# Hybrid attention block: the column factors of the attention output are applied in the output projection, with a longer probability ring and another step order

## What is computed

```python
def forgetting_attention(q, k, v, f_logit):      # "FoX": 8 heads of width 64
    c = cumsum(log_sigmoid(f_logit))
    s = q @ k.T * scale + c_i - c_j              # causal mask
    p = softmax(s); o = p @ v

def differential_attention(q, k, v, lam, g_sub, lam_init):   # 4 heads, values of width 128
    p1, p2 = softmax(q1 @ k1.T * scale + alibi), softmax(q2 @ k2.T * scale + alibi)
    o = (p1 - lam * p2) @ v
    o = rmsnorm(o, g_sub) * (1 - lam_init)

proj = rmsnorm(x, g_pre_mix) @ w_in              # q, k, v, forget logits of both kinds
mix = concat([fox, diff]) @ w_out
x = x + rmsnorm(mix, g_post_mix)
h = rmsnorm(x, g_pre_mlp)
x = x + rmsnorm(square(relu(h @ w_up)) @ w_down, g_post_mlp)
```

## Time and profile before

| | us |
|---|---|
| median of 3 runs | 3205.31 |
| the profiled execution, its time | 3201.39 |
| its span from the first to the last instruction | 3199.6 |
| PE busy in the span | 2935.2 (92%) |
| DVE busy | 1651.2 (52%) |
| POOL busy | 1030.2 (32%) |
| ACT busy | 1019.4 (32%) |
| mean granted TensorE clock | 0.963 |

### The profile page before, as it was taken

The page is one execution under the profiler, slowest core; times in us unless marked ns, Lnnn a source line. Parts: engine busy times, 40 slices in busy tenths (PEclk is TensorE's granted clock), DMA queues, the critical chain, the costliest instruction groups (busy, mean ns, idle before and its releaser), DMA issues. The chain is left out here.

```text
span 3199.6 us, 39104 instructions
## 1 busy us (share of the span) xinstructions
PE 2935.2 (92%) x13954; PEld 2420.8 (76%) x13954; DVE 1651.2 (52%) x2475; ACT 1019.4 (32%) x1974; POOL 1030.2 (32%) x734
## 2 busy tenths in 40 slices
PE   7999999688788798797797999999999999999996
PEld 5888888577677677676686788888887788888885
DVE  5111111379588588597454444444446544444446
ACT  4111111377577586585222111111112111111111
POOL 4220110158267267366111321222224322222224
PEclk9999999899899899899898999999999999999998
DMA  5342332744643644531663111101116111111112
GB/s 166 125 151 99 118 125 99 143 100 89 108 93 71 115 94 109 68 78 27 211 206 108 60 53 52 44 35 52 52 39 236 66 53 52 52 38 40 52 54 104
DMA packets 234969, 291.27 MB, mean 91 GB/s; under 512 B 37664, under 2 KB 160800, under 8 KB 234848
## 3 DMA queue, kind: packets, MB, share of 16 engines
q1 hardware_dynamic: 179984, 221.55, 26.9%
q10 hardware_dynamic: 54096, 67.38, 5.9%
q0 software_dynamic: 768, 0.79, 0.1%
HBM read 204.77 MB, written 84.90 MB: 91 GB/s over the span
## 5 line engine op out<-in xcount | busy, mean ns | idle before, releaser
L1873 DVE TENSOR_TENSOR ml_y<-ml_y,ml_ps_y 128x512 f32<-128x512 f32 x512 | 351.8, 687 | 233.6 <-PE ml_ps_y L1933 228.7
L1929 PE MATMUL ml_ps_y<-ml_dn_hi,ml_u_hi 128*128 128x512 f32 x1024 | 403.8, 394 | 11.5 <-DVE ml_y L1873 11.5
L1908 PE MATMUL ml_ps_u<-h_rows_hi,ml_up_hi 128*128 128x512 f32 x1024 | 400.0, 391 | 14.4 <-POOL ml_up_lo L1726 14.4
L1933 PE MATMUL ml_ps_y<-ml_dn_hi,ml_u_lo 128*128 128x512 f32 x1024 | 400.3, 391 | 0.0
L1931 PE MATMUL ml_ps_y<-ml_dn_lo,ml_u_hi 128*128 128x512 f32 x1024 | 399.9, 391 | 0.0
L1910 PE MATMUL ml_ps_u<-h_rows_lo,ml_up_hi 128*128 128x512 f32 x1024 | 399.7, 390 | 0.0
L1911 PE MATMUL ml_ps_u<-h_rows_hi,ml_up_lo 128*128 128x512 f32 x1024 | 399.5, 390 | 0.0
L1173 DVE TENSOR_REDUCE at_nmax<-at_ps_s 128x1 f32<-128x1024 f32 (+7 forms) x384 | 345.5, 907 | 83.0 <-PE at_ps_s L1272 77.4
L1849 DVE TENSOR_TENSOR ml_relu<-ml_relu 128x512 f32<-128x512 f32 x128 | 92.3, 721 | 496.6 <-ACT ml_relu L1812 496.6
L1726 POOL TENSOR_TENSOR ml_up_lo<-ml_up_raw,ml_up_hi 128x1024 fp32r<-128x1024 f32 x64 | 166.6, 2619 | 507.2 <-ACT ml_up_hi L1792 507.2
L1733 POOL TENSOR_TENSOR ml_dn_lo<-ml_dn_raw,ml_dn_hi 128x1024 fp32r<-128x1024 f32 x64 | 153.1, 2414 | 534.1 <-ACT ml_dn_hi L1802 534.1
(11 more groups left out here) (206 smaller groups left out, 5702.0 us busy)
## 6 DMA issues: line engine op xcount, KB each, us to landing
qk<-pj_out_sb ACTq DMA_DIRECT2D x64, 512.0 KB, 2.8
ml_up_raw<-in_w_up_dram SPq DMA_DIRECT2D x32, 1024.0 KB, 5.6
ml_dn_raw<-in_w_down_dram SPq DMA_DIRECT2D x32, 1024.0 KB, 7.6
at_q<-qk SPq DMA_DIRECT2D x96, 256.0 KB
at_k<-qk SPq DMA_DIRECT2D x96, 256.0 KB
vals<-pj_out_sb ACTq DMA_DIRECT2D x32, 512.0 KB, 3.0
at_v_sb<-vals SPq DMA_DIRECT2D x32, 512.0 KB, 8.1
pj_raw<-in_w_in_dram SPq DMA_DIRECT2D x24, 512.0 KB, 4.0
```

What stands on the lines that cost most here:

```text
L1873: dve.tensor_tensor(y[:, t, cols], y[:, t, cols], ps_y[:, b % 4, :], ALU.add)\
L1908: pe.matmul(ps_u[:, b % 4, :], up_hi[:, k, cols], h_hi[:, k, rows], start=(k == 0), stop=False)
L1929: pe.matmul(ps_y[:, b % 4, :], u_hi[:, s, f, rows], dn_hi[:, f, cols], start=(f == 0), stop=False)
L1933: last = pe.matmul(ps_y[:, b % 4, :], u_lo[:, s, f, rows], dn_hi[:, f, cols], start=False, stop=(f == FT - 1))
```

## The change

The multiplication by the column factors leaves `attend` and goes to `mix_out`. In `attend` the steps `row_in` and `o_scale` are gone, with the buffer `recips`. `store` is now made per block and not per pair (48 and not 32; a FoX block stores 64 partitions), right after its `o_add`; the ring `o_sb` has 2 slots, one per block, so `o_add` of block n waits for the store of block n - 2. `row_out` stays; the stage's end waits for its last writes. The memory that came free makes the probability ring 153 tiles long. The planner has a new table of urgencies and a new assumed cost of `fix`. In `mix_out`, per tile, three more loads bring the factors of 128 columns, spread over the partitions (512 KB in pieces of 512 bytes), into a single buffer, and DVE multiplies `m_raw` by them before the split.

```diff
-PROB_COLUMNS = 141 * 128
+PROB_COLUMNS = 153 * 128
-ORING = 3
+ORING = 2
-RUSH = {"score": -1.22, "max": -0.39, "corr": 0.1, "exp": 0.11, "fix": 0.34, "chain": -0.49, "mix": 0.53,
-        "turn": 0.12, "hi": 0.1, "lo": -0.23, "pv": 0.25}
-SPREAD, LEAD, EARLY = 1.06, 0.49, 0.72
+RUSH = {"score": -1.03, "max": -0.49, "corr": 0.43, "exp": 0.12, "fix": -0.47, "chain": 0.18, "mix": 0.47,
+        "turn": 0.12, "hi": -0.17, "lo": 0.04, "pv": 0.25}
+SPREAD, LEAD, EARLY = 1.14, 0.49, 1.63
...
-        finish([b], urgency)
-    def finish(pair, urgency):
-        q = pair[0].qb
-        walk.step("row_in", q, "SP", 0.6, urgency, ...)
-        walk.step("o_scale", q, "POOL", 1.3, urgency, [("row_in", q)] + [("o_add", b) for b in pair])
-        walk.step("store", q, "SP", 0.6, urgency, [("o_scale", q)], 6.0, line=("store", q % ORING))
...
-                walk.step("fix", (b.n, sc.a), "POOL", 2.0, at + RUSH["fix"], ...)
+                walk.step("fix", (b.n, sc.a), "POOL", 2.4, at + RUSH["fix"], ...)
...
         walk.step("o_add", b, "DVE", 0.69, end, [("o_half" if fox else "o_sq", b),
-                                                ("store", b.qb - ORING) if b.qb >= ORING else None])
-        if fox and b.s == 1:
-            finish([blocks[b.n - 1], b], end)
+                                                ("store", blocks[b.n - ORING]) if b.n >= ORING else None])
+        walk.step("store", b, "SP", 0.6, end, [("o_add", b)], 8.0, line=("store", b.n % ORING))
...
                 elif what == "store":
+                    b, cols = arg, slice(512 * arg.J, 512 * arg.J + 512)
+                    height = 64 if b.kind == FOX else P
+                    to = mixT[b.i, b.s * 64:b.s * 64 + 64, cols] if b.kind == FOX else mixT[b.i + 4, :, cols]
+                    sp.wait_ge(o_free, b.n + 1)
+                    sp.dma_start(to, o_sb[0:height, b.n % ORING, :]).then_inc(o_stored[b.n % ORING], 16)
...
+            for s in range(4):
+                sp.wait_ge(row_out[s], 16 * (len(blocks) // 4))
...
-                elif what == "o_scale":
-                    pool.wait_ge(row_in[q % 2], 16 * (q // 2 + 1))
-                    pool.wait_ge(o_free, pairs[q][-1].n + 1)
-                    pool.tensor_tensor(o_sb[:, q % ORING, :], o_sb[:, q % ORING, :], recips[:, q % 2, :], ALU.mult)
```

and in `mix_out`:

```diff
+            def load_factors(cols):
+                for half in range(2):
+                    sp.dma_start(factors[64 * half:64 * half + 64, 0:4], col_rows[0:4, half, cols].unsqueeze(0)
+                                 .to_broadcast([64, 4, P])).then_inc(factors_loaded, 16)
+                sp.dma_start(factors[:, 4:8], col_rows[4:8, 0, cols].unsqueeze(0).to_broadcast([P, 4, P]))\
+                  .then_inc(factors_loaded, 16)
+
+            load_mix(0, slice(0, P))
+            load_factors(slice(0, P))
             for k in range(KT):
                 sp.dma_start(w_raw[k], w_out[0, k * P:(k + 1) * P, :]).then_inc(w_loaded[k], 16)
...
+            load_mix(1, slice(P, 2 * P))
+            sp.wait_ge(m_scaled, 1)
+            load_factors(slice(P, 2 * P))
             sp.dma_start(xin[:, 1, :], x[0, P:2 * P, :]).then_inc(x_loaded[1], 16)
             with sp.Fori(0, LAST - 1) as i:
                 for s in range(2):
                     t = 2 * i + s + 2
                     sp.wait_ge(m_ready, t + 1)
+                    load_mix(s, bass.ts(t, P))
+                    sp.wait_ge(m_scaled, t)
+                    load_factors(bass.ts(t, P))
                     sp.wait_ge(y_step, 2 * (t - 1))
                     sp.dma_start(xin[:, s, :], x[0, bass.ts(t, P), :]).then_inc(x_loaded[s], 16)
...
             def split_mix(i, s, t):
                 dve.wait_ge(m_loaded[s], 16 * (i + 1))
+                dve.wait_ge(factors_loaded, 48 * (t + 1))
+                dve.tensor_tensor(m_raw[:, s], m_raw[:, s], factors[:, :, :], ALU.mult).then_inc(m_scaled, 1)
+                dve.wait_ge(m_scaled, t + 1)
                 dve.wait_ge(multiplied, t + 1)
                 dve.tensor_copy(m_hi[:, s], m_raw[:, s]).then_inc(m_hi_ready, 1)
```

More of the change, by code:

```diff
@@ L741, in attention_steps @@
             if sc.part and (fox or sc.s == 0):
-                walk.step("fix", (b.n, sc.a), "POOL", 2.0, at + RUSH["fix"], [("corr", sc), ("exp", parts[0])])
+                walk.step("fix", (b.n, sc.a), "POOL", 2.4, at + RUSH["fix"], [("corr", sc), ("exp", parts[0])])
             if not fox and sc.s == 1 and sc.part == sc.parts - 1:
@@ L798, in attend @@
     places, former = probability_columns(blocks)
-    pairs = [[b for b in blocks if b.qb == q] for q in range(blocks[-1].qb + 1)]
-    col_rows = nc.dram_tensor("col_rows", [KT, 2, S], F32).ap()
     fox_no = {b.n: n for n, b in enumerate(b for b in blocks if b.kind == FOX)}
@@ L900, in attend @@
         o_half_ready = r.sem("o_half_ready")
-        row_in = [r.sem(f"row_in{n}") for n in range(2)]
         o_free = r.sem("o_free")
-        o_scaled = r.sem("o_scaled")
         o_squared = r.sem("o_squared")
@@ L979, in _ @@
                       .then_inc(row_out[n % 4], 16)
[L980 to L991, removed]
-                elif what == "store":
[L993 to L996, removed]
+                elif what == "store":
+                    b, cols = arg, slice(512 * arg.J, 512 * arg.J + 512)
[3 more added lines that the diff above has]
+                    sp.dma_start(to, o_sb[0:height, b.n % ORING, :]).then_inc(o_stored[b.n % ORING], 16)
             for s in range(ORING):
-                sp.wait_ge(o_stored[s], 16 * ((len(pairs) + ORING - 1 - s) // ORING))
+                sp.wait_ge(o_stored[s], 16 * ((len(blocks) + ORING - 1 - s) // ORING))
+            for s in range(4):
+                sp.wait_ge(row_out[s], 16 * (len(blocks) // 4))
         @block.gpsimd
@@ L1319, in _, with mix_out @@
                     last.then_inc(x_ready, 1)
-def mix_out(nc, mixT, w_out, x, g_post_mix, g_pre_mlp, x2, h2T, rows_hi, rows_lo):
+def mix_out(nc, mixT, col_rows, w_out, x, g_post_mix, g_pre_mlp, x2, h2T, rows_hi, rows_lo):
     with ExitStack() as ctx:
@@ L1329, in mix_out @@
         m_raw = r.sb("m_raw", [P, 2, KT, P])
+        factors = r.sb("factors", [P, KT, P])
         m_hi = r.sb("m_hi", [P, 2, KT, P], F32R)
@@ L1351, in mix_out @@
         m_loaded = [r.sem(f"m_loaded{s}") for s in range(2)]
+        factors_loaded = r.sem("factors_loaded")
         x_loaded = [r.sem(f"x_loaded{s}") for s in range(2)]
+        m_scaled = r.sem("m_scaled")
         m_hi_ready = r.sem("m_hi_ready")
@@ L1376, in _, with load_mix @@
         def _(sp):
-            sp.dma_start(m_raw[:, 0], mixT[:, :, 0:P].rearrange("k p n -> p k n")).then_inc(m_loaded[0], 16)
+            def load_mix(s, cols):
+                sp.dma_start(m_raw[:, s], mixT[:, :, cols].rearrange("k p n -> p k n")).then_inc(m_loaded[s], 16)
+            def load_factors(cols):
[6 more added lines that the diff above has]
+            load_factors(slice(0, P))
             for k in range(KT):
@@ L1382, in _ @@
             sp.dma_start(xin[:, 0, :], x[0, 0:P, :]).then_inc(x_loaded[0], 16)
-            sp.dma_start(m_raw[:, 1], mixT[:, :, P:2 * P].rearrange("k p n -> p k n")).then_inc(m_loaded[1], 16)
+            load_mix(1, slice(P, 2 * P))
+            sp.wait_ge(m_scaled, 1)
+            load_factors(slice(P, 2 * P))
             sp.dma_start(xin[:, 1, :], x[0, P:2 * P, :]).then_inc(x_loaded[1], 16)
@@ L1388, in _ @@
                     sp.wait_ge(m_ready, t + 1)
-                    sp.dma_start(m_raw[:, s], mixT[:, :, bass.ts(t, P)].rearrange("k p n -> p k n"))\
-                      .then_inc(m_loaded[s], 16)
+                    load_mix(s, bass.ts(t, P))
+                    sp.wait_ge(m_scaled, t)
+                    load_factors(bass.ts(t, P))
                     sp.wait_ge(y_step, 2 * (t - 1))
@@ L1954, in hybrid_block @@
         rows_lo = r.sb("rows_lo", [P, KT, S // 2], F32R)
-        mix_out(nc, mixT, w_out, x, g_post_mix, g_pre_mlp, x2, h2T, rows_hi, rows_lo)
+        mix_out(nc, mixT, col_rows, w_out, x, g_post_mix, g_pre_mlp, x2, h2T, rows_hi, rows_lo)
         mlp(nc, rows_hi, rows_lo, h2T, w_up, w_down, x2, g_post_mlp, out)
```

23 lines of the change are left out of this document (9 added, 14 removed).

## The result

The changed kernel is slower: 3305.57 us median of 4 runs (3298.32 to 3306.40) against 3207.14 us (3201.39 to 3214.30, four runs by now) before, a ratio of 1.0301, 95% interval 1.0274 to 1.0327. The forecast was 3153 us and faster. The profiled execution took 3274.73 us (span 3273.0), 31 us less than the median of its timed runs; what those 31 us are is not known. It took 73 us more than its counterpart before, where the medians lie 98 us apart, so 25 us of the loss are in no view shown here.

The account below looks back on a forecast made before the run. No engine was full in attention, with PE and DVE near it; PE set mix_out's pace. Terms -45 - 10 + 3 + 0 - 7.4 + 4 + 3 = -52.4 us gave 3153 us from the median, range 3125 to 3208.

Parts of the forecast that it names:

- the last one of the steady state: mix_out's later tiles: factors, issued with 9.3 us left, land like m_raw in 5.5 to 7.7 us, so in time.
- the third: Rival in mix_out: factors landing after 9.3 us make every tile wait; 3219 us at a landing of 14; chance 0.06.
- Terms A and B: Attention: PE idle at o_add (40.3 us) and through POOL (19.1 us) would go; three quarters, 45 us, gained.
- C: Attention: PE's granted clock, lowered behind seven stalls, would mostly recover; 10 us gained, between 0 and 20.5.
- term D: Attention: o_add waits for the store two blocks before, only the longest landings late; 3 us lost, 0 to 10 per place.
- The list of what would show it: Signs expected in the profile after, such as attention's clock at 0.94 or more and mix_out tiles of 11.9 to 12.1 us.
- Term E: Attention: longer probability ring costed at nothing and new order taken as 0 us; at most 87 us could be gained.
- The second rival: Attention: the new order brings scores of four differential blocks too early, pushing back products; 68 us lost, 3221 us; chance 0.08.
- The seam: Between attention and mix_out: the stage ends once the last row write has landed; 7.4 us gained, bounds 6 and 9.
- The start: mix_out's start and second tile: added load issues and DVE's product delay PE; 4 us lost, bounds 2 and 8.
- The steady product: mix_out's steady tiles: DVE's added 1.23 us product leaves 0.35 us uncovered per two tiles; 3 us lost, bounds 0 and 9.

Follow-up runs that it names:

- the fastest kernel: Changed kernel with factors packed by three DRAM copies into 2048-byte pieces, old order tables and fix cost, probability ring of 141: 3143.63 us, ratio 0.9896.

## Why the prediction was wrong, step by step

**The step that failed** is the last one of the steady state: "the loads of `m_raw`, of the same size and with the same pieces of 512 bytes, landed in 5.5 to 7.7 us. They are in time by 1.6 us or more." Size and pieces were the same, but the bytes weren't: `m_raw` reads different bytes for each partition, the factors the same 512 bytes for 64 or 128 partitions. Measured are 17.2 us (last load), and the run with different bytes gives 4.2 us. So DVE waited in each of the 14 tiles of the steady state, 119 us in all, where the prediction had no wait. The nearest row was near in all but the one property that decided. Nothing in the trace before showed many such small shared pieces at once: the large shared reads of these stages, `row_in` and the gains of the norms, brought each partition one piece of 2048 or 4096 bytes, and four short vectors at the start of attention one of 256 bytes each.

**The rival that came true** is the third, "slower, by late factors", with a chance of 0.06. It gave 3219 us at a landing of 14 us. At 17.2 us its own rule (landing less 9.3 us, 14 tiles) gives 111 us more than the forecast, 3264. The prediction's mechanism, a wait in every tile from 9.3 us on, was right, and its reason for it, a DMA share of 0.58 already, was not: with different bytes the share is 0.69 and the loads are in time. Of the 42 us up to the measured 3306, 27 lie between the profiled executions and the medians and are in no view. The other 15 are chiefly the start with its second tile (28 us instead of 4) and attention (47 instead of 52), less 11 us by which the rule is too high for the 14 tiles.

**Terms A and B, with C (-55 us).** Right in kind: no wait of DVE on a store above 5.7 us, the chain through POOL gone, the clock at 0.95. In size they are open. Attention, with term D in it (-52), is 47.4 us shorter in the first pair of profiles and 20.7 in the pair from the other chips, both with the worse order. There PE's waits on `o_add` were a third shorter to begin with. With the old order and no factors the whole change gains 0.0132, 42 us. That the forecast came near in the first pair is partly luck: it left out the order, which cost 15 us.

**Term D (+3 us, two-slot ring).** DVE waits 15.1 us on stores in five places, PE 18.0 us on `o_add`. The list of what would show it asked for no DVE idle over 3 us and no PE wait over 5 us; one place misses both (5.70 and 6.16 us, near 656), two more miss the first (5.14 and 3.10 us of DVE). Mis-sized, within its bounds.

**Term E (0 us, order and ring).** The ring was right. The order was taken as 0 "for want of a row on either side" and cost 15 us, by two pairs of runs that agree. The second rival had the mechanism, DVE's work for the next differential block ahead of what ends the block before; as far as the timelines show, the work is not the score parts' maxima but the `mix` on DVE, 4 us in each of the four places and not 17, so it doesn't decide by itself.

**The seam (-7.4 us).** Measured -8.4, and -7.1 in the pair from the other chips, within its bounds of 6 and 9.

**The start (+4 us, with the second tile).** Measured +15.0 to the first product and 13.2 more to the second tile's, 28 us. With different bytes it is 3.3 us (11.1 against 7.8) and 2.3 more, against the kernel without factors: 5.6, within the bounds of 2 and 8. The term was nearly right but for the shared reads, which also hold up the weights behind them.

**The steady product (+3 us).** 0.8 us for two tiles were measured and not 0.35, so 5 to 6 us over 14 tiles: twice the term, within its bounds of 0 and 9. From the first product to that of mlp it is 215.0 us without factors, 220.8 with factors loaded once and 218.2 in the fastest kernel.

## What to carry to other kernels

A landing time may be borrowed from another load only if the source's addresses match too: who reads which bytes matters as well as how many and in what pieces. A value that all partitions need was cheap here in few long pieces: packing them first, by three copies, took 0.0347 or 110 us off. When a change comes with a new order of steps, the order is a change of its own: here it cost 15 us of what the rest gained. And a gain read from one pair of profiles on one chip (47 us in attention) may be half as large on the next (21).

## What the runs showed of the hardware

- Factors in 1024 pieces of 512 bytes a tile, where 64 or 128 partitions read the same addresses, land in 17.2 us (third load), and `m_raw` beside them in 17.1 and not 6.6; the same pieces from different addresses land in 4.2 us, and 256 pieces of 2048 bytes from shared addresses in 5.1 in the packed kernel with the old order and the ring of 141:

```profile
DMA to landing us min/median/max: 3.4/5.1/8.4
```

- While this goes on, the busy share of the transfer engines hardly tells: in mix_out it is 0.61 at 146 GB/s in the changed kernel, 0.69 at 208 GB/s with different bytes. The rate beside the share shows it.
- SP stands in the issue of the 64-partition loads for 3.9 us in the median and 11.7 at most when two buffers of factors are asked for, where the changed kernel has 0.6 in the median.
- The same program, the kernel before, took 3207 us where the change was measured and 3172 to 3177 on two other chips; PE's waits on `o_add` were 42.1 us in the first profile and 29.0 in that of chip 9.
